# First expert-weight loads issued four quarters at a time at fewer release points, one row part loaded earlier

## The reference

```python
h = h + mixed @ w_out[l]
h = h + hier_moe(rms_norm_2(h, norm2_gain[l]), w_route_group[l], ..., w_gate[l], w_up[l], w_down[l])
# per expert block:
hdn = jax.nn.silu(xblk @ w_gate[e]) * (xblk @ w_up[e])
return hdn @ w_down[e]
```

## Time and profile before

| | us |
|---|---|
| median of 3 runs | 1007.21 (1005.79 to 1007.43) |
| the profiled execution, its own time | 1006.36 |
| its span, first to last instruction | 1004.2 |
| PE busy | 874.0 (87%) |
| DVE busy | 447.9 (45%) |
| ACT busy | 331.9 (33%) |
| mean granted TensorE clock | 0.937 |

### The profile page before, as it was taken

One profiled execution on the slowest core, in us unless ns is written; L12 is line 12 of the kernel. 1 busy time (PEld: TensorE's weight loads), 2 busy tenths in 40 slices (PEclk: granted clock), 3 DMA queues, 4 the chain that ended last, 5 costly groups with the idle time before them and its releaser, 6 DMA issues.

```text
span 1004.2 us, 16158 instructions
## 1 busy us (share of the span) xinstructions
PE 874.0 (87%) x6998; PEld 604.3 (60%) x6998; DVE 447.9 (45%) x578; ACT 331.9 (33%) x433; POOL 22.0 (2%) x35
## 2 busy tenths in 40 slices
PE   9999999999999999999989988767867775786785
PEld 7889988888888889989979533211312221131232
DVE  6776878677876448898756310000100010010011
ACT  6476664665555328644523300000000000000002
POOL 0420000000000000000100000000000000000000
PEclk9999999999999999999999998787888898798898
DMA  9893325576645546352369999999999999999995
GB/s 323 256 358 131 144 86 168 168 250 208 208 169 179 198 155 222 131 205 85 109 186 386 373 415 403 429 427 428 428 429 428 428 428 428 428 428 428 424 426 221
DMA packets 75968, 294.34 MB, mean 293 GB/s; under 512 B 5247, under 2 KB 32655, under 8 KB 62592
## 3 DMA queue, kind: packets, MB, share of 16 engines
q1 hardware_dynamic: 70352, 283.91, 72.6%
q10 hardware_dynamic: 4128, 6.34, 1.8%
q0 software_dynamic: 1424, 3.16, 1.1%
HBM read 290.25 MB, written 4.10 MB: 293 GB/s over the span
## 4 chain that ended last, share of the span: by engine, by line
PE 64%; DMA 27%; DVE 5%; issue 1%; SPq 1%; ACT 1%; DVEq 0%; ACTq 0%
DMA arena<-in_w_down 10%; DMA arena<-in_w_gate 9%; DMA arena<-in_w_up 9%; PE psum L1271 8%; PE psum L1960 7%; PE psum L1134 6%; PE psum L1136 6%; PE psum L1135 6%; PE psum L1298 4%; PE psum L1273 4%; PE psum L1988 4%; PE psum L1635 2%; PE psum L1941 2%; PE psum L1171 1%; PE psum L1170 1%; PE psum L1168 1%
## 5 line engine op out<-in xcount | busy, mean ns | idle before, releaser
L1960 PE MATMUL psum<-arena,featL 128*32 128x512 f32 x1008 | 158.6, 696 | 61.0 <-DMA arena<-in_w_up 35.1
L2543 DVE TENSOR_TENSOR ring_rounded<-arena,hi_rounded 128x2048 fp32r<-128x2048 f32 x75 | 171.3, 2289 | 60.6 <-ACT hi_rounded L2087 59.3
L2087 ACT ACTIVATE hi_rounded<-arena 128x2048 fp32r<-128x2048 f32 x76 | 144.8, 1912 | 85.9 <-DMA arena<-in_w_down 18.0
L1960 PEld LDWEIGHTS psum<-arena,featL 128*32 128x32 f32 x1008 | 38.1, 124 | 169.2 <-issue 86.3
L1271 PE MATMUL psum<-ffn_in_rounded,hi_rounded 128*128 128x512 f32 x352 | 122.6, 395 | 0.7 <-DVE ffn_in_rounded L2535 0.7
L1988 PE MATMUL psum<-arena,featT 128*32 128x512 f32 x424 | 78.0, 733 | 35.5 <-DMA arena<-in_w_down 31.2
L1134 PE MATMUL psum<-hi_rounded,featT_rounded 128*128 128x256 f32 (+1 forms) x336 | 104.1, 310 | 0.8 <-DVE ring_rounded L2543 0.7
L1136 PE MATMUL psum<-hi_rounded,featL_rounded 128*128 128x256 f32 (+1 forms) x336 | 101.8, 303 | 0.0
L1135 PE MATMUL psum<-ring_rounded,featT_rounded 128*128 128x256 f32 (+1 forms) x336 | 101.8, 303 | 0.0
L1273 PE MATMUL psum<-ffn_in_rounded,ring_rounded 128*128 128x256 f32 x352 | 97.6, 277 | 0.0
L1271 PEld LDWEIGHTS psum<-ffn_in_rounded,hi_rounded 128*128 128x128 f32 x352 | 66.0, 188 | 16.2 <-DVE ffn_in_rounded L2535 1.0
(11 more groups left out here) (369 smaller groups left out, 1284.6 us busy)
## 6 DMA issues: line engine op xcount, KB each, us to landing
arena<-in_w_down SPq DMA_DIRECT2D x32, 2048.0 KB, 17.1
arena<-in_w_gate SPq DMA_DIRECT2D x28, 2048.0 KB, 20.6
arena<-in_w_up SPq DMA_DIRECT2D x24, 2048.0 KB, 24.1
arena<-in_w_in SPq DMA_DIRECT2D x14, 2048.0 KB, 8.9
arena<-in_w_up SPq DMA_DIRECT2D x25, 1024.0 KB, 9.0
arena<-in_w_gate SPq DMA_DIRECT2D x14, 1024.0 KB, 5.6
arena<-in_w_down SPq DMA_DIRECT2D x7, 1024.0 KB, 10.4
arena<-in_w_out SPq DMA_DIRECT2D x3, 2048.0 KB, 8.1
```

The lines of the kernel that those rows point to most:

```text
L1960: ins = mm(psum[32 * j:32 * j + 32, MB[4 + m], :], xg[:, 4 * half + k, 32 * j:32 * j + 32], weights(m, half, j, 512 * k), start=half == 0 ...
L2087: fn(high, view, ACT.Copy).then_inc(hi_ready, 1)
L2543: tt(low, view, high.bitcast(F32), ALU.subtract).then_inc(lo_ready, 1)
```

## The change

Seven places (`SPACED`) that were loaded quarter by quarter, each quarter behind its own fill, are loaded with their four quarters one right after another, and what a burst waits for is one point each: `ro`, P2, P4T, Re, HT, G2, Q, WT. `SPLIT` place 3 is cut into four parts of 512 floats instead of three parts; its first two parts (`ret_gn`, `late`) are issued behind P4T, the third (`rw_gn`) where the first two were, and the fourth where the last was.

```diff
-                 3: (final_gain, late[:], spent[:, LE["GT"][0]:LE["gap"][1]])}
+                 3: (row("ret_gn"), late[:], row("rw_gn"), spent[:, LE["GT"][0]:LE["gap"][1]])}
...
-                    first_load(2, 0, ("mat", "A", 1), ("natl", "V", 1), ("vraw", 1, 1), *inv(("P2", 1)))
-                    first_load(2, 1, *inv(("P3", 1), ("P4T", 1), ("H1", 0), ("H1", 1)))
+                    first_load(2, 0)
+                    wait_filled(sp, "inv", "P2", 1)
+                    first_load(2, 1)
+                    wait_filled(sp, "inv", "P4T", 1)
+                    wait_emptied(sp, "mat", "A", 1)
+                    first_load(NQ + 2, 3, hi=2)
                     wait_emptied(sp, "mat", "Aak", 1)
-                    first_load(NQ, 0, ("gn", 1), ("inv", "N", 1), ("mat", "Ro", 1), ("inv", "HT", 1))
-                    first_load(3, 3, *inv(("G1", 0), ("G1", 1), ("G2", 0), ("G2", 1)))
+                    wait_filled(sp, "mat", "Re", 0)
+                    first_load(NQ, 0)
+                    wait_filled(sp, "inv", "HT", 0)
+                    first_load(3, 3)
                     sp.wait_ge(mixed_ready, 1)
-                    first_load(2, 2, *inv(("TT", 0), ("TT", 1)), ("Q", 0), ("Q", 1))
-                    first_load(NQ, 1, ("U", 0, 1), ("WT", 0), ("WT", 1), ("St", 0))
-                    first_load(3, 2, ("U", 1, 1), ("St", 1), ("U", 2, 1), ("St", 2))
+                    wait_filled(sp, "inv", "G2", 0)
+                    first_load(2, 2)
+                    wait_filled(sp, "Q", 0)
+                    first_load(NQ, 1)
+                    wait_filled(sp, "WT", 1)
+                    first_load(3, 2)
                     wait_emptied(sp, "U", 1, 0)
-                    first_load(NQ + 2, 3, hi=2)
+                    first_load(NQ + 2, 3, lo=2, hi=3)
                     sp.wait_ge(mixed_ready, NT)
                     sp.wait_ge(u_first, NCH - 1)
                     first_load(2, 3)
...
-                    first_load(NQ + 2, 3, lo=2)
+                    first_load(NQ + 2, 3, lo=3)
```

## The result

| | before | after |
|---|---|---|
| median of 20 runs, us | 1006.11 (1003.79 to 1009.2) | 1008.82 (1005.97 to 1013.35) |
| ratio, 95% interval | | 1.0033 (1.0023 to 1.0043) |
| the profiled execution, its own time | 1006.36 | 1011.25 |
| its span | 1004.2 | 1009.1 |

The change costs 2.7 us. The profiled execution of after is one of its slower ones, 2.4 us above the median, so what follows adds up to the 4.9 us of its span, not to 2.7.

What follows compares the result with a forecast made beforehand. PE's progress up to 615 us was taken to bound the kernel. Stalls of 1.7 plus 0.35 for the slow spell, 2.05 against 2.69 us, gave 0.6 us less: median 1006.6, range 1003.6 to 1009.6.

Steps and rivals of the forecast that it cites:

- the same four terms: Page stalls expected after the change: HT 0.2, G2 0.4, Q 0.8 and place (2, 3) 0.3, together 1.7 us.
- What bounds the kernel: Up to 615 us PE's progress opens the weight stream; PE's gains before 577 us move the end, earlier bytes bring 0.
- What the issue pieces are: Chain, 480 to 530 us: PE standing for late pages of 256 instructions; 0.36 and 1.62 us fell under loads.
- Their floor: A page takes at least 3.6 us from the border before it (1.4 + 0.9 + 1.3); Q loses at least 0.3.
- a sign against itself: The prediction called itself wrong if a page stalls PE where the loads are idle.
- The early bursts at nothing: Bursts at ro, P2, P4T and Re, 0.3 us or more behind their borders: 0 to 0.2 us each, taken as 0.
- HT 0.2, G2 0.4, Q 0.8: Page stalls in us from the bursts at these fills; ranges 0 to 0.6, 0 to 0.9 and 0.3 to 1.8.
- WT at 0: Burst at WT, 0.5 us ahead of a border whose page takes PE 8.4 us: a late fetch is covered, 0.
- Place (2, 3) at 0.3, upper bound 1.3: 1 MB cell moved forward to the border of 524.7: 0 if the fetch passes, 1.3 us behind the whole cell.
- The prediction's own sign: It called itself wrong if the page of 524.7 makes PE stand for over a microsecond.
- The slow spell: PE at a granted clock of 0.80 until 524.71, costing 0.71 us; it stays or goes, so half, 0.35, was taken.
- The rival with 5.3 us of stalls and 1009.8 us: Fetches inside bursts fare worse: four pages at upper ends, 4.6 us, plus slow spell 0.7; 2.6 us more; chance 0.20.

Runs made afterwards that it cites:

- e4: Changed kernel, but no cell loaded between the fills ro and Y 1, all of it issued behind Y 1; 1020.84 us, ratio 1.0149.
- e10: e9 with its four late cells released one fill later, behind the border (HT 1, G2 1, Q 1, St 0); 1002.98 us, ratio 0.9968.
- e1: Changed kernel with only the bursts up to Re; from HT on the quarters are spread as before; 1006.33 us, ratio 1.0007.
- e14: The changed kernel itself again, on the same chip as e13 and e15; 1010.22 us, ratio 1.0040.
- e5: Changed kernel with one wait more: place (2, 3) also waits for the fill Y 0; 1007.10 us, ratio 1.0010.
- e2: Changed kernel with only the bursts from HT on; the quarters before are spread as before; 1010.52 us, ratio 1.0053.
- e3: Changed kernel with its four late bursts released one fill later, behind the border; 1007.15 us, ratio 1.0019.
- e13: e15 with each cell as four quarters of 256 KB again, released behind the border, place (2, 3) held until Y 0; 1005.12 us, ratio 0.9998.
- e8: Changed kernel with each of the seven places loaded by one DMA of 1 MB, same release points; 1008.19 us, ratio 1.0017.
- e9: e8 with place (2, 3) also waiting for the fill Y 0, as in e5; 1004.70 us, ratio 0.9984.
- e6: Changed kernel, early bursts kept, from HT on spread quarters one or two fills earlier than in e1, none between Q 0 and St 0; 1005.02 us, ratio 0.9997.
- e7: As e1, but from HT on quarters issued in pairs, at the later fill of the two or one fill on; 1005.52 us, ratio 0.9994.
- e15: e10 once more, on the same chip as the changed kernel e14; 1002.98 us, ratio 0.9974.
- e11: Kernel before with the first two parts of place 3 issued early, right behind the last quarter at H1; 1006.28 us, ratio 1.0001.
- e12: e11 with the two parts held until the fill H2 tile 1, behind the border; 1007.45 us, ratio 1.0012.

## Why the prediction was wrong

The forecast was 0.6 us less than before, and it came out 2.7 us more. The measured 1008.8 us lies within the stated range (1003.6 to 1009.6), but the direction was wrong. The sum of the stalls after was to be 1.7 us; in the profile the same four terms are 0.87 + 1.33 + 2.16 + 2.3 = 6.7 us.

**What bounds the kernel** held. PE's lateness at the logits came out at the end nearly in full (5.4 and 4.9 us in the profiles), and bytes loaded earlier brought nothing. It holds in one direction only: e4 shows that bytes loaded later cost their full time.

**What the issue pieces are** held: pages of 256 instructions whose fetch is late under loads. e4 and e10 show it from both sides. Their floor did not: the 3.6 us for a page to come, and with it the 0.3 us that Q's burst was to cost in any case, were taken from the one page at 490. With no loads at all (e4) the packet starts 0.9 us behind the border for the pages at Q and in St, and 1.8 us for that at G2, and none of them made PE stand. The page of 493 made it stand 0.85 us with the loads idle, which the prediction had named as a sign against itself; why that page alone comes late is open.

**The early bursts at nothing** held within the noise (e1); single profiles show up to 0.61 us at 490.

**HT 0.2, G2 0.4, Q 0.8** is the step that failed, together with place (2, 3) below. The mechanism was the one named, the sizes were 0.87, 1.33 and 2.16 us, each above its upper bound (0.6, 0.9, 1.8); in e14, the same kernel, 1.56, 0.79 and 2.16.

What was wrong is the rule behind them: "a burst released at the border or up to half a microsecond behind it lets the fetch go first". It does not follow from its own numbers, since a burst's first packets start 0.9 us after the issue and the fetch 1.4 us behind the border. In e5 the burst of G2 came 0.2 us behind the border, and 1.06 MB, the rest of HT's and most of G2's, passed before the instruction packet; in e2, 0.6 us behind it, PE stood the same 1.95 us. Nor was a burst over in 3.5 us: that of Re, issued from 499.56, was to run until 503.3, but 1.04 MB had passed only at 505.2, and 0.84 MB went by without an instruction packet between 502.5 and 506.0. Even released some 1.1 us behind the border, quarters left the page in St 1.3 us late (e3, e13), and one DMA of 1 MB did not make it late (e8).

I also took the borders of G2, Q and WT by the times of before, as 0.1 behind, level with and 0.5 us ahead of the fill. But these fills are the last ones ahead of the border in the program's order. A late page moves the border and not the fill, so a burst can be issued far ahead of it (0.9, 1.4 and 2.7 us). It is tempting to say that each late page makes the next one later. The Q page speaks against it. Its packet started 3.5, 4.1 and 4.2 us after the issue of G2's burst in e5, after and e14, wherever the border was. With G2's page in time PE stood 1.95 us there (e5), with that page 0.87 us late 1.33 us (after), and with it 1.56 us late 0.79 us; the chain of e14:

```profile
507.66 1.56 issue
...
513.35 0.79 issue
```

What a stall loses there is in part won back at the next border. The page in St, at 1.89 to 2.71 us in the same runs and e2, shows no such order. What sets its size is open.

**WT at 0** held: its page has 8.4 us.

**Place (2, 3) at 0.3, upper bound 1.3**, is the term that missed by most: PE stood 2.3 us. The upper bound let the fetch wait for this cell alone; it came 4.3 us behind the border, after 1.11 MB, more than the cell. The prediction's own sign, a page of 524.7 that makes PE stand for over a microsecond, came true. e5 and e9 take this piece away.

**The slow spell**: it stayed in after (0.79), as half of my term said, and in e14, where it begins later (columns as in the earlier trace rows):

```profile
521.50:525.50 4.00, 3.73 (x52) 2.98 (x48) 1.92 (x4) 0.97 (x2) 0.00 (x0) 0.57 0.47 148
```

Held against the standstill in St ahead of it, the profiles give an order. Behind 1.12 us or less (e1, e6, e7, and e4, e8, e9, e10, e15) the granted clock was 1.00 up to 528 us. Behind 1.36 us and more (e13, before, e5, after, e14, e2) it fell to 0.50, the lower of its two levels, for some microseconds. Behind 1.34 us it fell in e11 and e12 and not in e3.

The rival with 5.3 us of stalls and 1009.8 us came within a microsecond of the measured 1008.8. I gave it 0.20, and the forecast, with middle values for each page, 0.35. Its terms were the right ones at their upper ends, but 4.6 us of stalls are still too few for the profile's 6.7; that the time fits so well is in part luck, since the profiled execution is 2.4 us above the median.

## What to carry to other kernels

On a path of many small instructions, the fetch of the next instruction page is a load with a deadline: count the instructions, find the borders, and see that the load queue is short when a border is passed. When spread loads are gathered, look first at the loads behind them: they move forward too, onto borders of their own, and here that cost the most. One DMA for a cell did better here than four quarters at the same point. Releasing a load by the first event behind the border and not by the last one ahead of it gave 1.2 to 1.6 us in each of three pairs, none of them clear by itself.

## What the runs showed of the hardware that was not expected

- One DMA of 1 MB in 8 KB packets delays an instruction fetch less than four DMAs of 256 KB in 2 KB packets with the same data: 2.1 us in the whole time (e15 against e13). It is over sooner, and in e10 the instruction packet started as soon as it was through; whether that is the reason is not shown.
- How long an instruction packet waits differs much: in e10 it started within 1.9 us of the border, in the gap between two loads, behind 0.4 to 0.6 MB; in after only 3.5 us behind a border, under 0.84 MB, with loads still passing. By the Trainium skill (DMA: Bandwidth & Descriptors, Queues, rings and completion order) an engine takes turns between its queues packet by packet; the 0.84 MB in after do not agree with that, and e10 does not bear on it, since little else was passing when its packet started. What the packet waits for is open.
- The page at 493 us was 0.30, 0.57 or 0.85 us late in most profiles, the last of these in e4 too, which had no loads there.
- Executions of the kernel before spread over 5 to 7 us on each chip (1002.58 to 1009.45 on one).
